# Turning the last modulation chunk of a group behind the first row of the next group

## The reference

```
sh1, sc1, gt1, sh2, sc2, gt2 = split(silu(c) @ w_mod[i] + b_mod[i], 6)        # and the same with c_ctx
p = (rmsnorm(x) * (1 + sc1) + sh1) @ w_in[i]
x = x + gt1 * rmsnorm(concat(gla(p), short_conv(p)) @ w_out[i])
x = x + gt2 * rmsnorm(ffn(rmsnorm(x) * (1 + sc2) + sh2))                      # gains of the norms left out
```

## Time and profile before

| | |
|---|---|
| median of 3 runs | 1744.21 us (1742.09 to 1745.59) |
| the profiled execution | 1743.79 us, span 1742.0 us |
| busy share of the span | TensorE 94%, VectorE 55%, ScalarE 31% |
| mean granted TensorE clock | 0.986 of full speed |
| data read | 473.6 MB, 272 GB/s over the span |

### The profile page before, as it was taken

How to read it: one execution, slowest core, us unless ns; L and a number is a source line. 1 busy time by engine, 2 the same in 40 slices (tenths; PEclk the granted TensorE clock), 3 DMA queues, 4 the chain that set the end, 5 groups by cost and what they waited for, 6 DMA issues and landing times.

```text
span 1742.0 us, 21264 instructions
## 1 busy us (share of the span) xinstructions
PE 1640.8 (94%) x8432; PEld 1123.7 (65%) x8432; DVE 954.8 (55%) x1343; ACT 536.9 (31%) x682; POOL 4.0 (0%) x13
## 2 busy tenths in 40 slices
PE   6999999999999999998999999999989999888886
PEld 3788675788888885797788833887338873333322
DVE  4588775544445776698698712986129951110102
ACT  4421243400000005414577501774027730000001
POOL 0000000000000000000000000000000000000000
PEclk9999999999999999999999999999999999999999
DMA  9320785333321326327599999999999999999996
GB/s 361 135 97 1 285 296 192 99 97 97 97 97 37 133 70 223 115 80 290 230 376 376 346 391 408 412 408 412 414 407 412 409 407 405 408 412 409 410 415 270
DMA packets 160619, 476.26 MB, mean 273 GB/s; under 512 B 10002, under 2 KB 33012, under 8 KB 146164
## 3 DMA queue, kind: packets, MB, share of 16 engines
q1 hardware_dynamic: 158688, 474.24, 71.0%
q10 hardware_dynamic: 1812, 0.41, 0.1%
HBM read 473.58 MB, written 1.05 MB: 272 GB/s over the span
## 4 chain that ended last, share of the span: by engine, by line
PE 71%; SPq 12%; DMA 6%; DVE 5%; issue 3%; ACT 2%; ACTq 0%; DVEq 0%; POOL 0%; POOLq 0%
PE ps L914 10%; PE ps L915 10%; PE ps L916 10%; SPq L781 10%; PE ps L1372 7%; PE ps L1364 6%; PE ps L1366 6%; PE ps L1272 6%; DMA ring<-in_e_w 4%; SPq L785 2%; PE ps L1312 2%; PE ps L878 2%; PE ps L837 2%; DMA ring<-in_w_in 1%; PE ps L1218 1%
## 5 line engine op out<-in xcount | busy, mean ns | idle before, releaser
L1272 PE MATMUL ps<-ring,work 128*64 128x512 f32 x1040 | 259.7, 612 | 35.7 <-DMA ring<-in_e_w 28.8
L2530 DVE TENSOR_TENSOR norms<-work,ps 64x256 f32<-64x256 f32 x70 | 29.7, 424 | 327.7 <-ACT work L1835 326.2
L1272 PEld LDWEIGHTS ps<-ring,work 128*64 128x64 f32 x1040 | 83.9, 141 | 184.7 <-issue 181.6
L914 PE MATMUL ps<-ring_rounded 128*128 128x512 f32 (+1 forms) x536 | 190.6, 356 | 2.9 <-DVE norms L2312 1.6
L1974 DVE TENSOR_TENSOR ring_rounded<-ring,hT_rounded 128x2048 fp32r<-128x2048 f32 x77 | 174.3, 2286 | 18.9 <-ACT hT_rounded L1858 18.8
L916 PE MATMUL ps<-ring_rounded 128*128 128x512 f32 (+1 forms) x472 | 163.3, 346 | 0.0
L1858 ACT CAST hT_rounded<-ring 128x2048 fp32r<-128x2048 f32 x77 | 146.4, 1915 | 33.2 <-PE ps L1366 19.0
L916 PE MATMUL ps<-mixT_rounded,ring_rounded 128*128 128x512 f32 x328 | 127.6, 389 | 0.0
L1312 PE MATMUL ps<-ring,mixT 128*64 128x512 f32 x520 | 118.0, 596 | 4.6 <-DMA ring<-in_e_w 4.4
L914 PE MATMUL ps<-mixT_rounded,work_rounded 128*128 128x512 f32 x304 | 118.3, 389 | 0.0
L915 PE MATMUL ps<-hT_rounded,work_rounded 128*128 128x512 f32 x304 | 118.3, 389 | 0.0
(11 more groups left out here) (295 smaller groups left out, 2713.6 us busy)
## 6 DMA issues: line engine op xcount, KB each, us to landing
ring<-in_e_w SPq DMA_DIRECT2D x311, 1024.0 KB, 18.3
ring<-in_w_mod SPq DMA_DIRECT2D x24, 2048.0 KB, 11.2
mixT<-in_e_w SPq DMA_DIRECT2D x25, 1024.0 KB, 18.4
ring<-in_w_in SPq DMA_DIRECT2D x12, 2048.0 KB, 8.8
ring<-in_w SPq DMA_DIRECT2D x22, 1024.0 KB, 7.9
ring<-in_w_out SPq DMA_DIRECT2D x4, 2048.0 KB, 15.5
ring<-in_w SPq DMA_DIRECT2D x4, 2048.0 KB, 7.7
ring<-in_w SPq DMA_DIRECT2D x2, 1536.0 KB, 9.6
```

The lines of the kernel that those rows point to most:

```text
L914: pe.matmul(acc, w_high_, x_high_, start=first, stop=False)
L1272: ins = pe.matmul(narrow_bank(b)[H * w:H * w + H, :], xsel[:, k, 0:H], piece_words(e, pair[w])[:, at_:at_ + BLK], start=(k == 0), stop=(k ...
```

## The change

Nine of the twelve groups (`LATE`) no longer turn their last chunk themselves. It is turned in the group that follows in the program, right behind that group's first row product. `turned_at(place)` gives the chunks whose columns are turned at a place; TensorE's `mods`, the bank plan and VectorE's `take_mods` calls use it. ScalarE's `take_rows` calls stay as they are, and so do the banks handed to each group and the order of the loads. What is turned where:

| place | rows | columns before | columns after |
|---|---|---|---|
| keys | (0,4) (0,5) | (0,4) (0,5) | (0,4) |
| added | (0,6) (0,7) | (0,6) (0,7) | (0,5) (0,6) |
| states | (0,8) (0,9) | (0,8) (0,9) | (0,7) (0,8) |
| outputs | (0,10) (0,11) (1,0) | (0,10) (0,11) (1,0) | (0,9) (0,10) (0,11) |
| residual | (1,1) (1,2) | (1,1) (1,2) | (1,0) (1,1) |
| entry | (1,3) | (1,3) | (1,2) |
| second | (1,4) (1,5) | (1,4) (1,5) | (1,3) (1,4) |
| entry1 | (1,6) | (1,6) | (1,5) |
| keys1 | (1,7) (1,8) | (1,7) (1,8) | (1,6) (1,7) |
| states1 | (1,9) | (1,9) | (1,8) (1,9) |

`start` and `last` are as before. The diff, with the calls that only exchange `MODS[...]` for `turned_at(...)` cut to three:

```diff
+LATE = {"added": "keys", "states": "added", "outputs": "states", "residual": "outputs", "entry": "residual",
+        "second": "entry", "entry1": "second", "keys1": "entry1", "states1": "keys1"}
+
+def turned_at(place):
+    chunks = MODS[place]
+    if place in LATE.values():
+        chunks = chunks[:-1]
+    if place in LATE:
+        chunks = MODS[LATE[place]][-1:] + chunks
+    return chunks
...
-        chunks = MODS[place]
-        for n, ch in enumerate(chunks):
+        turns = iter(turned_at(place))
+        for n, ch in enumerate(MODS[place]):
             use(("mrow", *ch), nxt(), ("mod", *ch))
-            if n:
-                use(("mcol", *chunks[n - 1]), nxt())
-        use(("mcol", *chunks[-1]), nxt())
+            if n or place in LATE:
+                use(("mcol", *next(turns)), nxt())
+        for ch in turns:
+            use(("mcol", *ch), nxt())
...
             def mods(place):
-                chunks = MODS[place]
-                for n, ch in enumerate(chunks):
+                turns = iter(turned_at(place))
+                for n, ch in enumerate(MODS[place]):
                     mod_rows(*ch)
-                    if n:
-                        mod_cols(*chunks[n - 1])
-                mod_cols(*chunks[-1])
+                    if n or place in LATE:
+                        mod_cols(*next(turns))
+                for ch in turns:
+                    mod_cols(*ch)
...
-                    accs = {h: begin(("o", L, h), 2 * L + i) for i, h in enumerate(heads)}
+                    accs = {h: begin(("o", L, h), (1 + len(turned_at("states1"))) * L + i) for i, h in enumerate(heads)}
...
-                    take_mods(*MODS["entry1"])
+                    take_mods(*turned_at("entry1"))
...
-                take_mods(*MODS["states1" if L else "states"])
+                take_mods(*turned_at("states1" if L else "states"))
...
-                    take_mods(*MODS["outputs"])
+                    take_mods(*turned_at("outputs"))
```

More of the change, by code:

```diff
@@ L2259, in _ @@
                                       ALU.mult).then_inc(state_ops, 1)
-                take_mods(*MODS["keys1" if L else "keys"])
+                take_mods(*turned_at("keys1" if L else "keys"))
                 conv(3)
                 if L == 0:
-                    take_mods(*MODS["added"])
+                    take_mods(*turned_at("added"))
                 dve.wait_ge(state_exp, 6 * L + 6)
@@ L2347, in _ @@
                 add_branch(2 * L, lambda k: ("y", L, k), c0)
-                take_mods(*MODS["residual" if L == 0 else "last"])
+                take_mods(*turned_at("residual" if L == 0 else "last"))
                 if L:
@@ L2355, in _ @@
                 if L == 0:
-                    take_mods(*MODS["entry"])
+                    take_mods(*turned_at("entry"))
                     for j in range(JF):
@@ L2376, in _ @@
                     add_branch(1, lambda k: ("y2", k), 0)
-                    take_mods(*MODS["second"])
+                    take_mods(*turned_at("second"))
             dve.wait_ge(iota2_done, 3)
```

## The result

| | before | after |
|---|---|---|
| median | 1745.07 us (1742.09 to 1747.11, 6 runs) | 1758.16 us (1756.30 to 1761.08, 6 runs) |
| profiled execution, span | 1743.79 us, 1742.0 us | 1756.30 us, 1754.5 us |
| mean granted TensorE clock | 0.986 | 0.980 |

The ratio is 1.0077, 95% interval 1.0063 to 1.0092: slower by 13.1 us of median, 12.5 us of span. The forecast was 11.3 us slower, 1755.5 us, with a range to 1758.5: the median lies inside, near its top. Of the 2.7 us between the forecast and the median 1.2 are in the profiled execution (12.5 for 11.3).

A forecast was written before the change was run, and what follows sets the result against it. TensorE was taken as busy nearly throughout, the experts' stage as bound by weight loads; terms -1.3 + 8.5 + 2.3 + 0.4 + 0.6 + 0.6 + 0 + 0.2 = +11.3 us gave a median of 1755.5 us, range 1751 to 1758.5.

The forecast's parts named there:

- residual: Layer 1's residual group: ScalarE's second copy and the squares behind it come 0.6 us later; cost 0.4 us, between 0 and 0.6.
- entry: Group entry: ScalarE's copy before its modulations also waits for the older chunk's transposes; cost 0.6 us, bounds 0.3 to 0.7.
- entry1: Group entry1: ScalarE's copy before its modulations also waits for the older chunk's transposes; cost 0.6 us, bounds 0.3 to 0.7.
- keys1 with states1: Groups keys1 and states1: the recurrence gains 0.4 us, states1 loses 0.6; cost 0.2 us, between -0.5 and 0.6.
- the routing: First part of the experts' stage, which was forecast to keep its length; no cost in the sum.
- The clock at outputs: TensorE's clock falls to half in the idle time at outputs; cost 2.3 us, from nothing to 2.5.
- o: Heads' output products after keys, added and states: start at 218.4, released by VectorE; gain 1.3 us, bounds 0.8 to 2.
- The stall at outputs: Columns 11 wait for bank 5 until VectorE reduces columns 9 behind head 3; cost 8.5 us, between 8 and 9.
- Rival 1: Whole kernel: VectorE reaches the columns in time everywhere, nine stalls go; -7.3 us, 1736.9, or 1738.5 with ScalarE costs; chance 4%.
- Rival 2: Outputs: the stall is there but absorbed, or products pass the transposes; +0.5 us, 1744.7; chance 4%.
- Rival 3: Outputs: the stall is there but the clock stays up; +9.0 us, 1753.2; chance 12%.
- Rival 4: Outputs: the stall is longer, VectorE's splits before the reduction wait for late weights, 1.2 us more; 1756.7; chance 12%.

The follow-up runs named there:

- Experiment 1: Changed kernel with outputs' bank list (4, 5, 6, 7, 4, 6) in place of (4, 5, 6, 7), so columns 11 meet row 11's bank: 1746.89 us, ratio 1.0011.
- experiment 2: Changed kernel, same banks, with VectorE reducing columns 9 ahead of head 0 instead of behind head 3: 1750.14 us, ratio 1.0032.
- experiment 4: Changed kernel, same banks, with ten extra matmuls nobody reads ahead of columns 11 to keep TensorE busy: 1757.51 us, ratio 1.0069.
- experiment 3: Kernel before with only one move, the last chunk of states turned in outputs, old bank list: 1755.07 us, ratio 1.0061.
- experiment 6: Kernel before with only the moves into entry and entry1: 1748.25 us, ratio 1.0015.
- experiment 5: Kernel before with only four moves, into added, states, outputs and states1, and outputs' bank list (4, 5, 6, 7, 4, 6, 4): 1744.05 us, ratio 0.9995.
- experiment 7: Changed kernel, all nine moves, with outputs' bank list (4, 5, 6, 7, 4, 6) and a second buffer for the copied row: 1741.40 us, ratio 0.9984.

## Why the prediction was right in its mechanism, and which step failed

**The step that failed is the part of the sum behind outputs.** It gave residual, entry, second, entry1 and keys1 with states1 1.8 us together, and the routing nothing ("The experts' stage keeps its length"). Measured are 4.0 us: 0.7, 0.6, 0, 1.3, 0.25 and 1.2. The largest term is the routing's, which the sum put at nothing; the next is the stretch at half clock in entry1. The clock at outputs was off the other way, 1.4 us for 2.3, and o gained 0.2 less. That the whole came to 12.8 for 11.3 is in part luck, since 2.2 us too few behind outputs stand against 0.9 too many in the clock.

**The stall at outputs: right in mechanism, place and size.** Forecast: columns 11 wait for bank 5, 8.5 us, reduction reached behind head 3. The wait is 9.42 us where 9.7 were forecast; TensorE and VectorE both came there 1 us earlier, as the gain before it had shifted them. Experiment 1 removes it by the bank alone, experiment 2 by VectorE's order alone, and experiment 4 prices it at 8.5 us with the clock up.

**The clock there: right that it falls, too dear.** 2.3 us were forecast from the 4.4 and 5 us of work until it came back after the two idle times in the earlier trace rows; it was 1.4, since here it came back 3.0 us after the work resumed. In experiment 3, 5.5 us of work were slow after a like idle time. The forecast took the earlier trace rows for a second case of an idle time that lets the clock fall, and it is none: in the window from 863.50 to 864.00 us the granted clock was already 0.56, with TensorE busy for all of the 0.50 us, and the idle time of 1.92 us came later. Only the case in the earlier trace rows bore on it. The bounds, nothing to 2.5, held for the kernel after; what decides between 3 and 5 us no run shows.

**o: right.** Forecast -1.3 and a start at 218.4 released by VectorE; the start is at 218.51, 1.2 us early, and 1.1 are left behind the first products. I had reckoned with the bank, not with the weights: row 9's products waited 0.55 us for their load now that TensorE came early, a wait that the wait behind them covers.

**residual: 0.7 for 0.4.** This lies above the bound of 0.6. The copy itself moved back by 0.7, and the squares' products, which wait for ScalarE one by one, took all of it over; I had let a part be absorbed. Experiments 1 and 2 have the same 0.7. **entry: right**, 0.6. **second and keys1 with states1: right**, 0 and 0.25.

**entry1: 1.3 for 0.6.** The step of the copy is right: experiments 1, 2 and 6 have 0.6 us there. The rest, 0.66, is the stretch at half clock behind it.

The idle time in front of it is longer than before. Before, and after:

```profile
688.16 0.36 PE L924 MATMUL ps<-ring_rounded 128*128 128x256 f32 x1 [0.36 <-ACT ring_rounded L1622]
...
698.79 0.36 PE L939 MATMUL ps<-ring_rounded 128*128 128x256 f32 x1 [1.81 <-ACT ring_rounded L1637]
```

Of five executions with the 1.81 us (after twice, experiments 1, 2 and 4) four had the stretch right behind it, of the eight without it (before twice, experiments 3, 5 and 6, the kernels with a second buffer) none. That speaks for the change as its cause but does not show it.

**The routing: 1.2 for nothing.** "The experts' stage keeps its length" did not hold for its first part, the routing. The stretch at half clock there was 10.5 us long in the profile before and 14 in both of after. With entry1's 0.7 this is 1.9 us, more than the whole distance between forecast and profile, 1.5 us (12.8 against 11.3). Whether it belongs to the change stays open. Both executions of after lost 1.2 there, but the second of before lost 0.8 with no change at all, and over the twelve profiles behind the first one the same piece came out between 0.6 us shorter (experiments 6 and 7) and 1.2 us longer; experiment 4, with all nine moves, was 0.5 shorter. The times of before spread from 1742.1 to 1751.8, those of after from 1756.3 to 1761.1.

**The rivals.** Rival 1, faster by 7.3 us, fell with the stall; but experiments 1 and 5 show that it was also wrong in itself, since without the stall the nine moves are not faster (1.0011) and the four of experiment 5 gain nothing measurable (0.9995). Its price took nine stalls of 0.81 us; in truth each is worth that much only where nothing else sets the pace, which was so at keys and added. Rival 2 fell with the 9.42 us. Rival 3, clock up, 1753.2: the clock fell; made to stay up in experiment 4, it saved 1.4 us there, and the median did not move beyond the noise. Rival 4, late weights: VectorE was at its reduction 1.15 us earlier than before, so no weights held it up.

## What to carry to other kernels

When tiles are reordered in a fixed rotation of buffers, write down for every buffer who drains its previous tenant and when: one tile that came into a bank drained by VectorE in place of ScalarE cost 8.5 us, 9.9 with the clock, and two more numbers in the bank tuple took that back. A stall that comes from sharing one small buffer is better removed with a second buffer (-0.22% and -0.23% in two measurements) than with an order that hides it, since a new order makes the copies, and all that stands behind them, wait for more. And take more than one profile before a difference of 2 us in one stage is put down to a change.

## What was not expected of the hardware

- The same program on TensorE had stretches of 3.5 to 4 us at half clock (1.2 of 2.4 GHz) in one execution and not in the next: 676.5 and 785.5 us in the second profile of before. The engine was busy in 3.37 of 3.5 us and in all of 4.0 us there. In other kernels they stood at 314.5, 678.5, 686.5, 691, 699, 700, 787 us. Each cost 0.1 to 1.7 us. What brings them the runs do not show.
- 1.81 us of idle time before the first product of entry1's projections was followed at once by such a stretch in both executions of after and in experiments 1 and 4; in experiment 2, with the same idle time there, it was not. In experiment 2 an idle time of 2.13 us, ended at 236.4 us, was followed by such a stretch from 236.9 on.
- Before the clock fell, in the idle time of 9.4 us, some 2 us passed; after work resumed it took 3.0 us to come back here, 4.4 and 5 us in the earlier trace rows.
- Keeping TensorE busy through an idle time kept the clock at 1.00 there and did not measurably shorten the execution: 1757.51 for 1758.16 us, ratios 1.0069 and 1.0077 with intervals that overlap.
